# Down in blocks of 1024 features, each replaced in its place, with the block sums of u and W_down made in Up

## The chip, the cores and the metric

The kernel runs on one core of one Trainium2 chip. The metric is the device time of one execution in microseconds; it is 3420.22 us before the change, the median of 3 runs (3415.82 to 3422.02). [...]

## The reference

One layer of an encoder over 2048 rows of 1024 features:

```python
proj = rms_norm(h, g_mix) @ w_in                    # q, k, v of two groups of heads
h = h + concat(diff_attention, dilated_attention) @ w_out
hn = rms_norm(h, g_mlp)
h = h + square(relu(hn @ w_up)) @ w_down            # 1024 -> 4096 -> 1024
gate = sigmoid(rms_norm(h, g_ple) @ w_ple_gate)
h = h + gate * (p @ w_ple_proj)
return rms_norm(h, g_final)
```

The change touches the line with `w_up` and `w_down`, and the edges of the stages beside it.

## The kernel before

The stages run one after the other in one program with hand-written queues for each engine: projection, differential attention, dilated attention, `Mix` (W_out), `Up` (W_up), `Down` (W_down), `Gate`. Semaphores tie the queues; the order of the work on an engine is the order in its queue.

`Up` and `Down` use the Winograd form of Strassen's product: both operands are cut in 2 x 2 blocks, and 7 products of blocks (q = 0 to 6) stand for 8. Some of the 7 operands are blocks as they are, the others are sums and differences of blocks. Each product is made of 3 matmuls for every 128 of the contracted dimension (`matmul3`, lines 136 to 138: hi by hi, hi by lo, lo by hi). ScalarE copies an operand into its hi part (`hi_...`), another engine subtracts that from the operand for the lo part (`lo_...`).

`Up` takes the 2048 rows in two halves (z). The 7 operands of a half (`b_hi`, `b_lo`, made from the transposed rows `xt`, with the sums T1 to T4 in `add_t1` to `add_t4`) stay in SBUF for 16 steps. A step n takes 256 columns of W_up: `load_a` on SP, `sum_a` and `sum_s4` on POOL, `hi_a` on ScalarE, `lo_a` on VectorE, 84 matmuls on TensorE. ScalarE copies three of the products out of PSUM (`copy`) and makes the relu of one block; VectorE adds and squares the others (`y`: lines 1979 and 1981; the y of products 3, 4 and 5 are called y3, y4, y5 here). The four blocks of u = relu squared (u21, u22, u11, u12) are stored to DRAM by SP. Each y of a step waits until all four stores of the step before have landed (`stored`). The seventh product of a step waits for y4.

`Down` contracts the 4096 features. Before the change it takes 512 of them at a time: 2 halves of the rows x 8 groups of features x 2 = 32 passes k. A pass has 7 products q for two pairs of row tiles (s), each of 6 matmuls. u of a group comes in 4 pieces m, in four slots, as four blocks; POOL makes the sums (`sum_u`), ScalarE the hi part and VectorE the lo part of all seven at once. W_down of a group comes as four blocks in one of two slots; POOL makes the sums (`sum_w`), ScalarE the hi parts, VectorE three and POOL four of the lo parts (`lo_w`, line 2154). VectorE adds each product from PSUM to the residual rows `h` in SBUF (`add`, line 2322); TensorE's later products wait for these additions, since they add onto the same bank or reuse it. All DMAs of these stages are issued by SP.

`Gate` follows: W_ple_gate is scaled and split in the last two passes of `Down`.

## Time and profile before

| what | value |
|---|---|
| median of 3 runs | 3420.22 us |
| profiled execution, its own time | 3421.58 us |
| span from first to last instruction | 3419.8 us |
| TensorE matmul busy | 3161.2 us, 92% |
| TensorE weight load busy | 2706.2 us, 79% |
| VectorE busy | 2020.9 us, 59% |
| ScalarE busy | 1418.1 us, 41% |
| POOL (GpSimd) busy | 1396.8 us, 41% |
| granted TensorE clock, mean | 0.977 of full |

Matmuls are pipelined, so the busy time of TensorE adds up durations that overlap: its 0.39 us a matmul is longer than the distance from one to the next. The stages and the waits say more than the shares of the whole span.

### The profile page before, as it was taken

What the parts mean: (1) busy time and instruction counts of PE and PEld (TensorE: products, weight loads), DVE (VectorE), ACT (ScalarE), POOL (GpSimd) and SP (SyncE); (2) the same over time, 40 slices, a digit from 0 to 9 for tenths busy, and PEclk for the clock granted to TensorE, in tenths of its full rate; (3) what the DMA queues carried; (4) which work ended last, traced back from release to release, by engine and by line L of the source; (5) the groups of instructions that cost most, each with busy time, mean ns of one, the idle gap of its engine ahead of it and who ended that gap; (6) DMA issues with size and microseconds to landing.
All of it is one profiled execution on the core that took longest, in us unless ns stands there. A gap on an engine that the chain in (4) does not pass through costs nothing.

```text
span 3419.8 us, 48589 instructions
## 1 busy us (share of the span) xinstructions
PE 3161.2 (92%) x17504; PEld 2706.2 (79%) x17504; DVE 2020.9 (59%) x3415; ACT 1418.1 (41%) x2496; POOL 1396.8 (41%) x1052
## 2 busy tenths in 40 slices
PE   8999999999999999989979998999788868889998
PEld 8988888888888899977868886788676757767787
DVE  5134434888888756655555556555677747776222
ACT  4011112777777778852233333334232213233332
POOL 2133330011111167732342224323788868887322
PEclk9999999999999999999999999999999989999999
DMA  5233337003122168646634332233322242224221
GB/s 176 79 113 123 119 118 182 26 20 82 43 58 71 44 151 208 157 127 223 228 114 137 105 117 103 102 117 124 126 96 99 96 151 99 99 74 152 100 84 53
DMA packets 311341, 384.35 MB, mean 112 GB/s; under 512 B 79552, under 2 KB 225344, under 8 KB 305856
## 3 DMA queue, kind: packets, MB, share of 16 engines
q1 hardware_dynamic: 307760, 374.95, 35.8%
q10 hardware_dynamic: 3344, 6.29, 0.8%
q8 instruction: 142, 2.33, 0.3%
q14 instruction: 95, 0.78, 0.1%
HBM read 254.94 MB, written 126.22 MB: 111 GB/s over the span
## 4 chain that ended last, share of the span: by engine, by line
PE 68%; POOL 14%; DVE 7%; DMA 4%; ACT 4%; issue 3%; SPq 1%; POOLq 0%; DVEq 0%; ACTq 0%
POOL h_w_lo L2154 5%; PE a_acc L136 5%; PE a_acc L137 5%; PE a_acc L138 5%; PE c_pv L844 5%; PE e_acc L136 5%; PE e_acc L137 5%; PE e_acc L138 5%; PE b_pv L984 4%; PE c_turned L833 3%; PE c_scores L825 3%; PE c_scores L826 3%; PE b_scores L1236 3%; DVE c_neg_half L741 2%; DVE c_a_row L774 2%
## 5 line engine op out<-in xcount | busy, mean ns | idle before, releaser
L136 PE MATMUL h_acc<-h_w_hi,h_u_hi 128*128 128x512 f32 x896 | 361.9, 404 | 120.3 <-DVE h_h L2322 120.0
L741 DVE TENSOR_REDUCE c_neg_half<-c_scores 128x1 f32<-128x1024 f32 x256 | 312.7, 1222 | 83.5 <-PE c_scores L826 83.5
L138 PE MATMUL h_acc<-h_w_hi,h_u_lo 128*128 128x512 f32 x896 | 356.8, 398 | 0.0
L137 PE MATMUL h_acc<-h_w_lo,h_u_hi 128*128 128x512 f32 x896 | 356.3, 398 | 0.0
L2322 DVE TENSOR_TENSOR h_h<-h_acc,h_h 128x512 f32<-128x512 f32 x448 | 290.2, 681 | 87.0 <-PE h_acc L138 85.7
L136 PE MATMUL e_acc<-e_b_hi,e_a_hi 128*128 128x512 f32 x768 | 304.0, 396 | 38.0 <-DVE e_u L1979 21.7
L2196 ACT CAST h_u_hi<-h_u_raw 128x1792 fp32r<-128x1792 f32 x64 | 108.5, 1696 | 536.6 <-POOL h_u_raw L2182 536.6
L136 PEld LDWEIGHTS h_acc<-h_w_hi,h_u_hi 128*128 128x128 f32 x896 | 173.0, 193 | 176.3 <-issue 74.2
L698 ACT ACTIVATE c_e<-c_scores,c_neg_max 128x1024 f32<-128x1024 f32 x256 | 287.0, 1121 | 59.7 <-DVE c_neg_max L748 51.8
L137 PE MATMUL e_acc<-e_b_lo,e_a_hi 128*128 128x512 f32 x768 | 303.0, 395 | 0.0
L138 PE MATMUL e_acc<-e_b_hi,e_a_lo 128*128 128x512 f32 x768 | 302.7, 394 | 0.0
L844 PE MATMUL c_pv<-c_v,c_at 128*128 128x128 f32 x2048 | 270.1, 275 | 0.4 <-ACT c_o L712 0.4
L2201 DVE TENSOR_TENSOR h_u_lo<-h_u_raw,h_u_hi 128x1792 fp32r<-128x1792 f32 x64 | 174.7, 2729 | 129.4 <-ACT h_u_hi L2196 129.4
L844 PEld LDWEIGHTS c_pv<-c_v,c_at 128*128 128x128 f32 x2048 | 248.6, 192 | 0.5 <-ACT c_o L712 0.5
L665 POOL TENSOR_SCALAR c_mean<-c_ssq,c_eps 128x1 f32<-128x1 f32 x64 | 16.9, 264 | 546.4 <-ACT c_o_junk L719 515.7
L2154 POOL TENSOR_TENSOR h_w_lo<-h_w_raw,h_w_hi 128x1024 fp32r<-128x1024 f32 x64 | 203.2, 3206 | 84.0 <-ACT h_w_hi L2149 84.0
L825 PE MATMUL c_scores<-c_kt_hi,c_qs 128*128 128x512 f32 x512 | 224.6, 439 | 5.2 <-ACT c_e L698 5.1
L136 PEld LDWEIGHTS e_acc<-e_b_hi,e_a_hi 128*128 128x128 f32 x768 | 146.7, 191 | 71.8 <-DVE e_a_lo L1784 23.7
L826 PE MATMUL c_scores<-c_kt_lo,c_qs 128*128 128x512 f32 x512 | 203.5, 397 | 0.0
L138 PEld LDWEIGHTS h_acc<-h_w_hi,h_u_lo 128*128 128x128 f32 x896 | 172.4, 192 | 37.4
L137 PEld LDWEIGHTS h_acc<-h_w_lo,h_u_hi 128*128 128x128 f32 x896 | 173.4, 194 | 35.2
L706 ACT COPY c_at<-c_turned 128x512 f32<-128x512 f32 x256 | 149.8, 585 | 119.2 <-PE c_turned L833 117.3
(202 smaller groups left out, 8027.4 us busy)
## 6 DMA issues: line engine op xcount, KB each, us to landing
s_qkt<-a_hl SPq DMA_DIRECT2D x128, 256.0 KB, 2.8
e_a<-w_up_dram SPq DMA_DIRECT2D x64, 512.0 KB, 4.9
s_u<-e_u SPq DMA_DIRECT2D x128, 256.0 KB, 2.0
h_w_raw<-w_down_dram SPq DMA_DIRECT2D x64, 512.0 KB, 7.4
h_u_raw<-s_u SPq DMA_DIRECT2D x128, 256.0 KB, 3.4
b_kt<-s_qkt SPq DMA_DIRECT2D x64, 256.0 KB, 9.4
a_w_raw<-w_in_dram SPq DMA_DIRECT2D x24, 512.0 KB, 5.3
d_nd<-s_nd SPq DMA_DIRECT2D x48, 256.0 KB, 3.0
```

The source lines that it names most:

```text
L136: nc.tensor.matmul(out, lhs_hi, rhs_hi, start=first, stop=False, skip_group_check=onto)
L137: nc.tensor.matmul(out, lhs_hi, rhs_lo, start=False, stop=False, skip_group_check=onto)
L138: return nc.tensor.matmul(out, lhs_lo, rhs_hi, start=False, stop=last, skip_group_check=onto)
L698: nc.scalar.activation(e[:, n % 2, m, f * HALF:(f + 1) * HALF], bank(n, u), ACT.Exp, bias=neg_max[:, n % 2, m:m + 1], accum_out=sums[:, n ...
L706: nc.scalar.copy(at[:, n % 2, 4 * g:4 * g + 4].rearrange("p c t -> p (c t)"), turned[:]).then_inc(S["at"], 1)
L741: nc.vector.tensor_reduce(neg_half[:, m, f:f + 1], bank(n, u), AX.X, ALU.max, negate=True).then_inc(S["halved"], 1)
L825: nc.tensor.matmul(found, queries, kt_hi[h % 2][:, m, cols], start=True, stop=False)
L826: ins = nc.tensor.matmul(found, queries, kt_lo[h % 2][:, m, cols], start=False, stop=True)
L844: ins = nc.tensor.matmul(pv[:, :VD], at[:, s, c], v[h % 2][:, c], start=(c == 0), stop=(c == KT - 1))
L2154: op(self.w_lo[s][:, q], self.w_raw[s][:, q], self.w_hi[s][:, q].bitcast(F32), ALU.subtract).then_inc(S[sem], 1)
L2201: self.nc.vector.tensor_tensor(self.u_lo[s][:], self.u_raw[s][:], self.u_hi[s][:].bitcast(F32), ALU.subtract).then_inc(S["u_lo"], 1)
L2322: nc.vector.tensor_tensor(tile, bank[:], tile, ALU.add).then_inc(S["h"], 1)
```

## The change

`Down` takes 1024 features at a time: 4 groups of features, 16 passes, 12 matmuls to a product. There is one place for each of the 7 blocks of W_down and for each of the 7 blocks of u (two parts, s), no second slot. When product q of a pass is done, SP loads the next block of that q into the same place. POOL makes all lo parts of u, VectorE all lo parts of W_down. The additions to `h` are half as many, as a product holds twice the features.

The sums are no longer made in `Down`. In `Up`, POOL makes the block sums of u after u11 and after u12 (`sum_s`, eight operations of 128x256 a step), and SP stores seven blocks in place of four. In steps 18 to 25 of `Up` (`FIRST_T`), SP loads two parts of W_down a step (`load_t`), POOL sums the even and VectorE the odd ones (`sum_t`), and SP stores four sums of each to a new DRAM tensor `t` (`store_t`). The order of the queues in `Up` changes: u12's stores move behind the next step's loads, y4 stands ahead of the first two `lo_a`, T3 is made in the place of a half of `xt` and for the second half of the rows already at step 4, T1 comes from T2 in place too. `Gate` loads W_ple_gate in quarters during the last pass, and its buffers lie elsewhere.

```diff
     def add_t3(self, pool, z):
-        self.free_b(pool, z, 1)
-        self.nc.gpsimd.tensor_tensor(self.b_raw[1][:], self.half(1, 1), self.half(0, 1),
+        pool.wait_ge(self.S["xt_in"], 16 * self.HT * (z + 1))
+        self.nc.gpsimd.tensor_tensor(self.half(0, 1), self.half(1, 1), self.half(0, 1),
                                      ALU.subtract).then_inc(self.S["b_sum"], 1)
...
     def add_t1(self, dve, z):
-        if z == 0:
-            self.mix.wait_products(dve, TILES - 1)
-        self.free_b(dve, z, 4)
-        self.nc.vector.tensor_tensor(self.b_raw[4][:], self.half(0, 1), self.half(0, 0),
+        dve.wait_ge(self.S["b_sum"], 3 * z + 2)
+        dve.wait_ge(self.S["b_lo"], 5 * z + 1)
+        self.nc.vector.tensor_tensor(self.half(0, 0), self.half(1, 1), self.b_raw[2][:],
                                      ALU.subtract).then_inc(self.S["b_t1"], 1)
...
+    def load_t(self, sp, n):
+        for i in range(2):
+            sp.dma_start(self.t[n % 2][:, 2 * i:2 * i + 2].rearrange("p k d -> p (k d)"),
+                         self.D["w_down"][n * 256 + i * P:n * 256 + (i + 1) * P]).then_inc(self.t_in[n % 2], 16)
+
+    def sum_t(self, eng, op, n):
+        S, t, done = self.S, self.t[n % 2], self.t_sum[n % 2]
+        eng.wait_ge(self.t_in[n % 2], 32 * (n // 2 + 1))
+        op(t[:, 4], t[:, 1], t[:, 0], ALU.subtract).then_inc(done, 1)
+        eng.wait_ge(done, 4 * (n // 2) + 1)
+        op(t[:, 5], t[:, 3], t[:, 4], ALU.subtract).then_inc(done, 1)
+        op(t[:, 1], t[:, 3], t[:, 1], ALU.subtract).then_inc(done, 1)
+        eng.wait_ge(done, 4 * (n // 2) + 2)
+        op(t[:, 6], t[:, 2], t[:, 5], ALU.subtract).then_inc(done, 1)
+
+    def store_t(self, sp, n):
+        sp.wait_ge(self.t_sum[n % 2], 4 * (n // 2) + 4)
+        t = self.t[n % 2]
+        sp.dma_start(self.D["t"][n, :, 0], t[:, 1]).then_inc(self.S["t_stored"], 16)
+        sp.dma_start(self.D["t"][n, :, 1:], t[:, 4:]).then_inc(self.S["t_stored"], 16)
...
+    def sum_s(self, pool, n, j):
+        nc, S = self.nc, self.S
+        u1 = (self.u11, self.u12)[j][:].rearrange("p (i k t) -> p i k t", i=2, k=2)
...
+            pool.wait_ge(S["s_stored"], 32 * (2 * n + j))
+        base = 8 * n + 4 * j
+        nc.gpsimd.tensor_tensor(self.s12[:, :, 0], u1[:, :, 1], u2[:, :, 1], ALU.add).then_inc(S["s_sum"], 1)
+        pool.wait_ge(S["s_sum"], base + 1)
+        nc.gpsimd.tensor_tensor(self.s12[:, :, 1], self.s12[:, :, 0], u1[:, :, 0], ALU.subtract).then_inc(S["s_sum"], 1)
+        nc.gpsimd.tensor_tensor(u1[:, :, 1], u1[:, :, 0], u1[:, :, 1], ALU.subtract).then_inc(S["s_sum"], 1)
+        pool.wait_ge(S["s_sum"], base + 2)
+        nc.gpsimd.tensor_tensor(self.s4u[:], u2[:, :, 0], self.s12[:, :, 1], ALU.subtract).then_inc(S["s_sum"], 1)
+
...
+        FIRST_T = range(FB + 2, FB + 2 + FB // 2)
 
...
+            def pairs(n, j, first, last):
                 z, f = divmod(n, FB)
+                return self.D["u"][f, :, 4 * z + 2 * j:4 * z + 2 * j + 2, first:last]
+
...
+            def store_2(n, j, u, y):
                 sp.wait_ge(S["y"], 7 * n + y)
-                cols = slice(z * HT * P + j * 512, z * HT * P + (j + 1) * 512)
-                sp.dma_start(self.D["u"][f, i, :, cols], u[:]).then_inc(S["stored"], 16)
-
-            for n in range(STEPS):
-                if n + 1 < STEPS:
-                    self.load_a(sp, n + 1)
+                sp.dma_start(pairs(n, j, 2, 4), u[:].rearrange("p (i k t) -> p i k t", i=2, k=2)).then_inc(S["stored"], 16)
+
+            def store_1(n, j, u):
+                sp.wait_ge(S["s_sum"], 8 * n + 4 * j + 3)
+                sp.dma_start(pairs(n, j, 0, 2), u[:].rearrange("p (i k t) -> p i k t", i=2, k=2)).then_inc(S["stored"], 16)
+                sp.dma_start(pairs(n, j, 4, 6), self.s12[:]).then_inc(S["s_stored"], 16)
+                sp.wait_ge(S["s_sum"], 8 * n + 4 * j + 4)
+                sp.dma_start(pairs(n, j, 6, 7).rearrange("p i k t -> p i (k t)"), self.s4u[:]).then_inc(S["s_stored"], 16)
+
+            for n in range(STEPS - 1):
+                self.load_a(sp, n + 1)
+                if n == FB + 1:
+                    self.wait_xt_used(sp, 1)
+                if n in FIRST_T:
+                    m = 2 * (n - FIRST_T[0])
+                    if m:
+                        sp.wait_ge(S["t_stored"], 32 * m)
+                    self.load_t(sp, m)
+                    self.load_t(sp, m + 1)
+                if n == FIRST_T[-1] + 1:
+                    self.wait_t(sp)
+                    down.load_w(sp, 0, 0)
+                    down.load_w(sp, 0, 1)
+                if n:
+                    store_1(n - 1, 1, self.u12)
+                store_2(n, 0, self.u21, 2)
+                store_2(n, 1, self.u22, 4)
+                if n in FIRST_T:
+                    self.store_t(sp, m)
+                    self.store_t(sp, m + 1)
+                store_1(n, 0, self.u11)
...
+            n = STEPS - 1
+            store_1(n - 1, 1, self.u12)
+            self.wait_parts(sp)
+            down.load_u(sp, 0, 0)
+            self.wait_product(sp, 0)
+            down.load_w(sp, 0, 2)
+            down.load_u(sp, 0, 1)
+            self.wait_product(sp, 1)
+            down.load_w(sp, 0, 3)
+            self.wait_product(sp, 2)
+            down.load_u(sp, 0, 2)
+            down.load_w(sp, 0, 4)
+            store_2(n, 0, self.u21, 2)
+            self.wait_product(sp, 3)
+            down.load_w(sp, 0, 5)
+            store_2(n, 1, self.u22, 4)
+            self.wait_product(sp, 4)
+            down.load_w(sp, 0, 6)
+            down.load_u(sp, 0, 3)
+            self.wait_product(sp, 5)
+            for t in range(4):
+                down.load_h(sp, 0, t)
+            store_1(n, 0, self.u11)
+            self.wait_product(sp, 6)
+            down.load_u(sp, 0, 4)
+            store_1(n, 1, self.u12)
+            self.wait_last(sp)
+            for t in range(4, HT):
+                down.load_h(sp, 0, t)
+            self.wait_stored(sp)
+            down.load_u(sp, 0, 5)
+            down.load_u(sp, 0, 6)
...
+                    self.lo_b(dve, 1, 1)
                 y(n, 1, 3, self.u21, c, self.u2, 3)
+                y(n, 3, 4, self.u22, a, self.p7, 2)
                 if n == 0:
                     mix.h_out(dve, TILES - 1)
+                    mix.wait_xt(dve, TILES - 1)
+                if n == 0:
+                    y(n, 5, 5, self.u11, self.acc_b[:, 0], self.p1, 1)
                 if n + 1 < STEPS:
-                    self.lo_a(dve, n + 1, 0)
-                    self.lo_a(dve, n + 1, 1)
-                y(n, 3, 4, self.u22, a, self.p7, 2)
-                if n == 0:
-                    mix.wait_xt(dve, TILES - 1)
+                    for q in range(2):
+                        self.lo_a(dve, n + 1, q)
...
+                if n:
+                    y(n, 5, 5, self.u11, self.acc_b[:, 0], self.p1, 1)
                 if n + 1 < STEPS:
-                    for q in range(2, 5):
+                    for q in range(2, 6):
                         self.lo_a(dve, n + 1, q)
...
-                    down.begin_vector(dve, 1)
-                y(n, 5, 5, self.u11, self.acc_b[:, 0], self.p1, 1)
-                if n + 1 < STEPS:
-                    self.lo_a(dve, n + 1, 5)
                 square(n)
...
                 if n + 1 < STEPS:
                     self.lo_a(dve, n + 1, Q - 1)
+                if n in FIRST_T:
+                    self.sum_t(dve, nc.vector.tensor_tensor, 2 * (n - FIRST_T[0]) + 1)
...
-            for n in range(STEPS - 1):
-                if n + 1 == FB:
-                    self.add_t3(pool, 1)
-                self.sum_a(pool, n + 1)
+            for n in range(STEPS):
                 if n + 1 == FB:
                     self.add_t2(pool, 1)
                     self.add_t4(pool, 1)
-                if n == FB + 6:
-                    down.sum_w(pool, 0)
-                self.sum_s4(pool, n + 1)
-            down.begin_pool(pool)
+                if n + 1 < STEPS:
+                    self.sum_a(pool, n + 1)
+                else:
+                    down.begin_pool(pool)
+                if n == 4:
+                    self.add_t3(pool, 1)
+                if n in FIRST_T:
+                    self.sum_t(pool, nc.gpsimd.tensor_tensor, 2 * (n - FIRST_T[0]))
+                self.sum_s(pool, n, 0)
+                if n + 1 < STEPS:
+                    self.sum_s4(pool, n + 1)
+                self.sum_s(pool, n, 1)
...
-    HALVES, HT, FG = 2, TILES // 2, D_FF // 512
+    HALVES, HT, FG = 2, TILES // 2, D_FF // 1024
     GROUPS = HALVES * FG
     DPS = GROUPS * 2
-    PAIRS_Z = HT // 2
-    SLOTS = 4
-    Q = 7
+    Q, J = 7, 4
...
+        homes = (0, 16, 32, 48, 124.25, 140.25, 156.25)
+        self.w_raw = [place(kit, f"h_w_raw{q}", kb, [P, J, 512]) for q, kb in enumerate(homes)]
+        self.w_lo = [place(kit, f"h_w_lo{q}", kb, [P, J, 512], F32R) for q, kb in enumerate(homes)]
+        self.w_hi = [place(kit, f"h_w_hi{q}", kb + 8, [P, J, 512], F32R) for q, kb in enumerate(homes)]
+        homes = ((68, 72), (76, 188.5), (192.5, 196.5), (80, 84), (88, 92), (112, 116), (120, 64))
+        self.u_raw = [[place(kit, f"h_u_raw{q}_{s}", kb, [P, J, P]) for s, kb in enumerate(h)] for q, h in enumerate(homes)]
+        self.u_lo = [[place(kit, f"h_u_lo{q}_{s}", kb, [P, J, P], F32R) for s, kb in enumerate(h)] for q, h in enumerate(homes)]
+        self.u_hi = [[place(kit, f"h_u_hi{q}_{s}", kb + 2, [P, J, P], F32R) for s, kb in enumerate(h)]
...
+    def load_w(self, sp, r, q):
+        f = self.J * (r % self.FG)
+        if r:
+            self.wait_product(sp, 2 * r - 1, q, 1)
+        s, before = self.loads(r, q)
+        if before:
+            sp.wait_ge(self.w_in[s], 16 * before)
+        if q in (0, 5, 6):
+            i, k = (q + 1) // 7 + (q == 5), int(q == 6)
+            src = self.D["w_down"].rearrange("(f i p) d -> f i p d", i=2, p=P)[f:f + self.J, i, :, k * 512:(k + 1) * 512]
...
+            src = self.D["t"][f:f + self.J, :, (0, 2, 3, 1)[q - 1]]
+        sp.dma_start(self.w_raw[q][:], src.rearrange("j p d -> p j d")).then_inc(self.w_in[s], 16)
+
+    def hi_w(self, act, r, q):
+        s, before = self.loads(r, q)
+        act.wait_ge(self.w_in[s], 16 * before + 16)
+        self.nc.scalar.copy(self.w_hi[q][:], self.w_raw[q][:]).then_inc(self.S["w_hi"], 1)
+
+    def lo_w(self, dve, r, q):
+        dve.wait_ge(self.S["w_hi"], self.Q * r + q + 1)
+        self.nc.vector.tensor_tensor(self.w_lo[q][:], self.w_raw[q][:], self.w_hi[q][:].bitcast(F32),
+                                     ALU.subtract).then_inc(self.S["w_lo"], 1)
+
+    def load_u(self, sp, k, q):
+        f, half = self.J * (k // 2 % self.FG), 4 * (k // (2 * self.FG)) + 2 * (k % 2)
+        if k:
+            self.wait_product(sp, k - 1, q, 1)
+        n, before = self.loads(k, q)
+        if before:
+            sp.wait_ge(self.u_in[n], 32 * before)
+        for s in range(2):
+            sp.dma_start(self.u_raw[q][s][:], self.D["u"][f:f + self.J, :, half + s, self.POS[q]].rearrange("j p t -> p j t")
+                         ).then_inc(self.u_in[n], 16)
+
+    def hi_u(self, act, k, q, s):
+        n, before = self.loads(k, q)
+        act.wait_ge(self.u_in[n], 32 * before + 32)
+        self.nc.scalar.copy(self.u_hi[q][s][:], self.u_raw[q][s][:]).then_inc(self.S["u_hi"], 1)
+
+    def lo_u(self, pool, k, q, s):
+        pool.wait_ge(self.S["u_hi"], 14 * k + 2 * q + s + 1)
+        self.nc.gpsimd.tensor_tensor(self.u_lo[q][s][:], self.u_raw[q][s][:], self.u_hi[q][s][:].bitcast(F32),
+                                     ALU.subtract).then_inc(self.S["u_lo"], 1)
...
+                r, step = k // 2, k % (2 * FG)
+                for q in range(Q):
+                    if k + 1 < DPS:
+                        self.load_u(sp, k + 1, q)
+                    else:
+                        self.wait_product(sp, k, q, 1)
+                        gate.load_early(sp, q)
+                    if k % 2 and r + 1 < GROUPS:
+                        self.load_w(sp, r + 1, q)
+                    if q == 2 and 0 < k - 2 * FG + 2 < 3:
+                        first = 4 * (k - 2 * FG + 1)
+                        for t in range(first, first + 4):
+                            self.load_h(sp, 1, t)
...
+            for k in range(DPS - 1):
+                for q in range(Q):
+                    for s in range(2):
+                        self.hi_u(act, k + 1, q, s)
+                    if k % 2:
+                        self.hi_w(act, k // 2 + 1, q)
+            for c in range(KC):
+                gate.split_hi(act, c)
...
+                for q in range(Q):
+                    if k == 0 and q + 2 < Q:
+                        self.lo_w(dve, 0, q + 2)
+                    for s in range(2):
+                        add(k, q, s)
+                    if k % 2 and r + 1 < GROUPS and q >= 2:
+                        self.lo_w(dve, r + 1, q - 2)
+                    if k % 2 == 0 and k and q < 2:
+                        self.lo_w(dve, r, q + 5)
...
+            for k in range(DPS - 1):
                 for q in range(Q):
                     for s in range(2):
...
+                        self.lo_u(pool, k + 1, q, s)
+            for c in range(KC):
+                gate.split_lo(pool, c)
...
+                pe.wait_ge(S["u_lo"], 14 * k + 2 * q + s + 1)
...
+                for j in range(J):
+                    ins = matmul3(nc, out[:], self.u_hi[q][s][:, j], self.u_lo[q][s][:, j],
+                                  self.w_hi[q][:, j], self.w_lo[q][:, j], q in (0, 1, 5) and j == 0, j == J - 1,
+                                  q not in (0, 1, 5))
...
+    def load_early(self, sp, q):
+        if q < 4:
+            self.load_w(sp, q)
+        if q == 0:
+            self.load_h(sp, 0)
+            self.load_h(sp, 1)
+        elif q == 1:
+            sp.dma_start(self.e_raw[1][:], self.D["w_ple_proj"][P:]).then_inc(self.e_in, 16)
+            self.load_h(sp, 2)
...
+        elif q == 3:
+            self.load_h(sp, 3)
```

## Rows read from the trace of the kernel before

**Rows 1.** The windows view of Up and Down; its first line names the columns.

```profile
core 0: us, PE busy (x) PEld busy (x) DVE busy (x) ACT busy (x) POOL busy (x), PEclk, DMA share, GB/s
1757.60:2398.60 641.00, 603.51 (x2615) 496.83 (x2616) 370.92 (x452) 223.69 (x357) 207.96 (x143) 0.97 0.35 119
2398.60:3163.50 764.90, 644.58 (x2698) 515.39 (x2696) 521.42 (x558) 219.64 (x182) 611.48 (x376) 0.96 0.32 110
```

**Rows 2.** POOL's timeline in Up: s4, begun as a step's products end.

```profile
2044.92 1.29 POOL L1767 TENSOR_TENSOR e_s<-e_a 128x512 f32<-128x512 f32 x1 [6.95 <-PE e_acc L138]
...
2103.84 1.29 POOL L1767 TENSOR_TENSOR e_s<-e_a 128x512 f32<-128x512 f32 x1 [7.38 <-PE e_acc L138]
...
2199.04 1.29 POOL L1767 TENSOR_TENSOR e_s<-e_a 128x512 f32<-128x512 f32 x1 [6.90 <-PE e_acc L138]
...
2242.88 1.74 POOL L1767 TENSOR_TENSOR e_s<-e_a 128x512 f32<-128x512 f32 x1 [4.41 <-PE e_acc L138]
...
2376.16 1.50 POOL L1767 TENSOR_TENSOR e_s<-e_a 128x512 f32<-128x512 f32 x1 [6.45 <-PE e_acc L138]
```

**Rows 3.** The waits in Down: total us, times, longest.

```profile
ACT h_u_hi L2196 <- POOL h_u_raw L2182: 532.3, 62, 26.9
...
PE h_acc L136 <- DVE h_h L2322: 120.0, 50, 15.0
```

**Rows 4.** POOL's timeline in Down, one round of a group.

```profile
2830.73 0.75 POOL L2177 TENSOR_TENSOR h_u_raw<-h_u_raw 128x256 f32<-128x256 f32 x1
...
2841.07 12.70 POOL L2154 TENSOR_TENSOR h_w_lo<-h_w_raw,h_w_hi 128x1024 fp32r<-128x1024 f32 x4 [5.60 <-ACT h_w_hi L2149]
...
2875.57 0.74 POOL L2177 TENSOR_TENSOR h_u_raw<-h_u_raw 128x256 f32<-128x256 f32 x1
```

**Rows 5.** TensorE's timeline: Up's start, and after a stall in Down.

```profile
1772.44 0.76 PE L136 MATMUL e_acc<-e_b_hi,e_a_hi 128*128 128x512 f32 x1 [15.38 <-DVE e_u L1979]
...
2817.42 0.63 PE L137 MATMUL h_acc<-h_w_lo,h_u_hi 128*128 128x512 f32 x1
2817.84 0.63 PE L138 MATMUL h_acc<-h_w_hi,h_u_lo 128*128 128x512 f32 x1
```

**Rows 6.** Instructions grouped by line and shape: busy us, mean ns, idle before.

```profile
L2322 DVE TENSOR_TENSOR h_h<-h_acc,h_h 128x512 f32<-128x512 f32 x448 | 290.2, 681 | 87.0 <-PE h_acc L138 85.7
L1847 DVE TENSOR_TENSOR e_b_lo<-e_b_raw,e_b_hi 128x2048 fp32r<-128x2048 f32 x5 | 11.3, 2283 | 0.9 <-ACT e_b_hi L1840 0.9
L1840 ACT CAST e_b_hi<-e_b_raw 128x2048 fp32r<-128x2048 f32 x5 | 9.5, 1904 | 11.2 <-DVE e_b_raw L1815 5.7 <-POOL e_b_raw L1802 2.8 <-POOL e_b_raw L1794 2.7
L1757 POOL TENSOR_TENSOR e_a<-e_a 128x512 f32<-128x512 f32 x31 | 41.5, 1340 | 229.3 <-DMA e_a<-w_up_dram 229.3
L2154 POOL TENSOR_TENSOR h_w_lo<-h_w_raw,h_w_hi 128x1024 fp32r<-128x1024 f32 x64 | 203.2, 3206 | 84.0 <-ACT h_w_hi L2149 84.0
L2139 POOL TENSOR_TENSOR h_w_raw<-h_w_raw 128x1024 f32<-128x1024 f32 x16 | 38.5, 2405 | 1.3
L2177 POOL TENSOR_TENSOR h_u_raw<-h_u_raw 128x256 f32<-128x256 f32 x64 | 48.1, 752 | 56.0 <-DMA h_u_raw<-s_u 56.0
```

**Rows 7.** DMA: a store alone and 1775 to 1800; loads, 1781 to 1796, 2762 to 2768.

```profile
s_u<-e_u SPq DMA_DIRECT2D x128, 256.0 KB, 2.0
...
s_u<-e_u SPq DMA_DIRECT2D x6, 256.0 KB, 5.2
...
DMA packets 7312, 4.21 MB, mean 281 GB/s; under 512 B 124, under 2 KB 7311, under 8 KB 7311
...
DMA packets 1120, 2.28 MB, mean 380 GB/s; under 512 B 89, under 2 KB 723, under 8 KB 1119
```

**Rows 8.** SP's timeline, and two of its issue lines (ns min/median/max).

```profile
1760.22 1.38 SPq L1750 DMA_DIRECT2D e_a<-w_up_dram  x2
...
2047.62 0.93 SPq L1750 DMA_DIRECT2D e_a<-w_up_dram  x2
...
L1892 SPq DMA_DIRECT2D s_u<-e_u x10: 319/338/339, 2116.4 to 2157.3; - x10
...
L2132 SPq DMA_DIRECT2D h_w_raw<-w_down_dram x64: 373/470/1543, 2126.6 to 3076.6; - x64
```

375 lines of the change are left out of this document (110 added, 265 removed).

## The prediction

> **What bounds the kernel now.** I read the three last stages by their windows first, then the waits inside the slowest, then the timeline of the engine those waits name. Up (32 steps) takes 641.0 us, Down (32 passes) 764.9 us, and TensorE issues about as many matmuls in both [rows 1]. Up's undisturbed pace is seen between two of its POOL rows seven steps apart: (2376.16 - 2242.88)/7 = 19.04 us a step of 84 matmuls, 0.2267 us each [rows 2]. Down has 2688 matmuls too, so at that pace it would take 609.3 us. It loses 155.6 us, and nothing but waits can be the cause: TensorE waits 120.0 us for VectorE's h_h additions, and those queue behind h_u_lo, behind ScalarE's h_u_hi, which waited 532.3 us for POOL's sums of u [rows 3]. The second set of u sums of one group starts at 2830.73 and the same set of the next at 2875.57: POOL goes round in 44.84 us where two passes need 38.07 [rows 4]. Four h_w_lo alone are 12.70 us of it. So POOL bounds Down, with further stalls (the longest 15.0 us) at the start and where the halves change, and the matmuls after a long stall run at half pace (0.42 us apart, the lower of the clock's two levels) [rows 5].
>
> **Down after the change.** It has 16 passes of 168 matmuls, again 2688. A pass is 168 x 0.2267 = 38.1 us.
> POOL: all sums go; it makes 14 u_lo of 128x512 per pass. The nearest rows are 128x512 sums at 1.34 us and 128x1024 lo parts at 3.21, 1.6 per 512 [rows 6]: 19 to 23 us. Not a bound.
> VectorE: 14 additions x 0.68 = 9.5 us, and seven w_lo of 128x2048 in every second pass, 2.28 us each, 16.0 us [rows 6]: 25.5 of 38.1. Additions halve from 448 to 224.
> ScalarE: 14 u_hi at 0.6 (a quarter of the 1.90 for 128x2048, and 0.1 for what doesn't shrink) and seven w_hi at 1.90 [rows 6]: 22 us.
> DMA: a pass loads 3.67 MB of u in 512 B pieces and, every second pass, 7.34 MB of W in 2 KB pieces. Loads with 512 B pieces moved 4.21 MB in 15 us, 281 GB/s; pieces of 1 to 4 KB 380 GB/s [rows 7]. So 13.1 + 19.3 = 32.4 us of a 38.1 us pass, 13 in the other. Each block's place is free after its product, and the next block is wanted there 12 products later, 12 x 2.72 = 32.6 us; load 4.7 + 2, hi 3, lo 4 need some 14. If VectorE's w_lo waits for a late block, the additions behind it have 8 us (three products) before TensorE misses them.
> Entry: u blocks 5 and 6 must wait for the last stores, but are wanted only at +27 us. Blocks of q = 2 wait on POOL behind the last sum of u, and this behind stores queued after 2 MB of h: at about +13 against +10.9. I take 5 us, and 2 for the rest. Down: 609.3 + 7 = 616, **-149 us** (bounds: 0 more, and +40 if each of the 8 odd passes slips 5 us).
>
> **Up, the stalls that go.** At the start VectorE holds y4 behind lo_a(1), whose W_up load issues at 1760.22, and TensorE waits 15.38 us [rows 5, 8]. With y4 ahead, TensorE does the seventh product and waits then for the same load, landing near 1768, lo part 1769: step 1 starts near 1769 instead of 1775: -6. At the change of halves two steps take 58.92 us instead of 38.08 [rows 2], 20.8 lost to T3, T2, T4 on POOL and their split. T3 is made at step 4 and its hi and lo early; T2 and T4 still wait for products, T4 ends near +18 us of the step, sum_a behind it at +22, ScalarE's relu behind those at +26, where +21.8 was due: 5 us, with slow clock 8: -12. The POOL sum of W (2199.04 to 2242.88, 43.84 for 38.08) goes: -6. The last step: -2. Together **-26 us** (0 to -35).
>
> **Up, the stalls that come.** POOL gets eight sums of 128x256 a step at 0.75 (a quarter of a 1024's 2.4 to 3.2): 6 us beside 5.4. s4 now follows the sums of u11 (done near +3), so s4 is ready at +4.3, its lo part at +5.7, and load_a, which waits for it, issues near +5.8 of a step; u12's store follows it, lands near +11.3, and y3, due at +10.9, may start until 14.1 before TensorE waits. I take 0 for ordinary steps (bound +3 each over 20 steps).
> In steps 18 to 25 SP's queue closes a circle. y3 of step n+1 (and all y behind it) waits for all four stores of step n. u12's store stands behind load_t of step n+1; load_t waits until the t sums of step n have landed; their odd half waits for VectorE's sum_t. That is last in VectorE's step n, behind the lo part of s4: it runs in step n+1 after s4 (+4.3), hi and lo (+5.7) and its own four operations (4 x 0.8), near +9. Count from its end, E. SP: two t stores 0.9, three stores of u 1.0, two load_a 0.93 [rows 8]: 2.9. 1 MB of t lands at 0.5 + 1.3 + 2.7 = 4.5 (2.7 for 1 MB at 380 GB/s; 1.3 is what is left of a small store's 2.0 without its 0.7 of bytes). Four load_t issue until 6.4, 0.47 each [rows 8]. By then 2.74 MB were issued ahead and drain at +8.1, 2.1 MB of load_t at +13.5; u12's store lands near +15. y3 0.7, its square 1.1, y4 0.7: +17.6. y4's square, two lo_a, y5: +21. POOL sums u11: +24; s4: +25.2; hi and lo: +26.8; sum_t 4 x 0.8: +30. The circle is 30 us, not 19.04: +11 for seven turns. TensorE feels it at the seventh product of a step, due at 16.3 and let go at 9 + 17.6 = 26.6; step 26, with 2 MB of W_down in the same place, pays 10 once more, plus 2 for the slow clock: **+89 us**.
> What decides is whether a small store waits for loads issued before it. A store of u lands in 2.0 us alone; in the stretch with eight xt loads the six stores had a median of 5.2 [rows 7]. That shows queueing, though not its full length, since these stores were issued with only part of the 4 MB still outstanding. I take full queueing, for this is the only stretch of before in which a store follows megabytes of loads. The Trainium skill ("DMA: Bandwidth & Descriptors", Queues, rings and completion order) says that a ring's descriptors are consumed in order and that the semaphore's increment lands only after every earlier write of that DMA engine. By that rule u12 lands when load_t is in, so the term is +89; by a store that lands as fast as alone it would be +37.
> Bounds: if stores pass loads, u12 lands at 2.9 + 1.6 + 2 + 2.3 = 8.8, the circle is 24: 5 x 7 + 2 = +37. If VectorE and POOL hold each other up (h_w_lo 3.21 beside 2.4), 35 us: 16 x 7 + 16 = +128.
>
> **Gate.** This only moves. Its W comes in quarters in the last pass, at 5.4, 10.9, 16.3 and 21.8 us of it; ScalarE needs some 2 us (twice half of the 1.90) and POOL up to 3.2 for each of eight chunks [rows 6]; the last two, in near +29, are done near +36. Tiles 2 and 3 of h2 load earlier, worth at most the first few us: -2 (bounds -5 and 0).
>
> **Sum.** -149 - 26 + 89 - 2 = -88. The profiled execution took 3421.58 us (span 3419.8): 3333.6. The median of the runs, 3420.22, is 1.4 less: **3332 us**.
>
> **Rivals.**
> A, the t stores cost little: stores pass loads, or the landing is faster. For it: DMA peaks at 380 GB/s and is idle most of a step. Against: the queueing seen above. Circle at 24 us or no circle: 3420 - 177 + 37 = 3280, or 3243 with none.
> B, ordinary steps slip too: with 1.5 to 3 us of stall each over some 20 steps (u12's store later than 14.1), +30 to +60: 3362 to 3392. For it: VectorE's operations stretch beside POOL's. Against: 2.8 us of margin.
> C, slower: Down becomes bound by loads. u comes in 512 B pieces 28 KB apart, which no row has on the read side (xt's pieces were small on the chip's side alone). It must eat 88 us: 5.9 us a pass more, (616 + 95)/16 = 44.4; a pair moves 14.7 MB, so the queue would have to manage under 165 GB/s. Against: 281 to 380 in rows [rows 7]. Break-even is 88 us lost there; at 155 to 165 GB/s it gives 3430 to 3480.
> D, the change doesn't lift POOL's bound because VectorE waits for late w_lo and so TensorE for sums, 3 to 5 us a pass: +50 to +80, 3382 to 3412; the 8 us margin speaks against.
>
> **Chances.** Forecast 0.60, A 0.17, B 0.11, C 0.06, D 0.06. The range reaches to A's 3280 and a little under, and to B's upper part: 3275 to 3385. The measurement tells no change within 0.2%, 7 us. Faster 0.92, same 0.02, slower 0.06.
>
> **What would show it.** Down from first to last h_acc near 616 us, no wait of h_acc for h_h over 3 us, POOL under 65% there. Steps 19 to 26 near 30 us, others 19.04; there y3 waiting for a store of u, and load_t issued some 4.5 us after the last t store. Halves change with under 10 us lost. I am wrong if steps 19 to 26 stay at 19 to 22 us (A), if steps 5 to 14 grow (B), or if in Down h_u_hi waits for loads (C) or h_acc for h_h behind h_w_lo (D).

## The result, and the profile after

The changed kernel takes **3453.88 us**, the median of 4 runs (3451.6 to 3456.27), against 3419.75 for the kernel before (4 runs): a ratio of 1.0101, 95% interval 1.0084 to 1.0119. It is slower by 34 us, 1%, where 3332 was forecast. The profiled execution has a span of 3449.8 us, 30.0 more than before. I read the same views again, first the windows of Up and of Down (the columns are those of [rows 1]):

```profile
1757.00:2564.70 807.70, 638.77 (x2605) 511.11 (x2606) 443.98 (x478) 210.58 (x353) 488.98 (x409) 0.90 0.49 165
2564.70:3197.20 632.50, 613.00 (x2697) 507.08 (x2695) 290.53 (x278) 246.10 (x299) 406.56 (x240) 0.98 0.68 217
```

Down falls by 132.4 us against [rows 1], close to the -149 forecast. Up grows by 166.7 where +63 was forecast. What follows gives 3.7 back, what precedes 0.6: -132.4 + 166.7 - 3.7 - 0.6 = +30.0. So the question is Up. TensorE's waits in the changed kernel (total us, times, longest):

```profile
PE e_acc L136 <- DVE e_u L2077: 107.1, 13, 12.8
PE e_acc L136 <- ACT e_p L2016: 50.8, 28, 9.7
...
PE h_acc L136 <- POOL h_u_lo L2274: 19.5, 1, 19.5
PE e_acc L136 <- DVE e_a_lo L1789: 12.3, 3, 7.8
```

The first is the large wait at the seventh product that the prediction expected in a few steps. The second is short, 1.8 us on average, but comes 28 times: nearly every step. POOL's timeline gives the pace, s4 of steps 5, 15, 19 and 27, as [rows 2] did:

```profile
1873.10 1.71 POOL L1772 TENSOR_TENSOR e_s<-e_a 128x512 f32<-128x512 f32 x1
...
2086.69 1.74 POOL L1772 TENSOR_TENSOR e_s<-e_a 128x512 f32<-128x512 f32 x1
...
2196.02 1.74 POOL L1772 TENSOR_TENSOR e_s<-e_a 128x512 f32<-128x512 f32 x1
...
2461.00 1.74 POOL L1772 TENSOR_TENSOR e_s<-e_a 128x512 f32<-128x512 f32 x1
```

Ordinary steps: (2086.69 - 1873.10)/10 = 21.36 us, not 19.04. Steps with t: (2461.00 - 2196.02)/8 = 33.12 us, not 30. These rows also lack the "<-PE e_acc" of [rows 2]: POOL no longer begins s4 as a step's products end, it comes to it late, and s4 itself takes 1.72 instead of 1.29 us. From the distances of all 32 of these rows in both kernels, the increase of Up by part (us):

| part of Up | forecast | measured |
|---|---|---|
| start, up to s4 of step 1 | -6 | -6.1 |
| step 2 (eight loads of xt) | 0 | +13.3 |
| 18 ordinary steps | 0 | +46.5 |
| the two steps at the change of halves | -12 | +2.9 |
| steps 18 to 26 (t), with the POOL sum of W that goes | +83 | +114.2 |
| rest | -2 | -4.1 |

### The profile page after: what moved, and what is told of

It is laid out like the page before. It is cut to its first block, busy times and chain, and to the rows that moved or that the text cites. A ratio compares the mean times of both kernels' runs of the same rounds, so it can differ in the third digit from the quotient of the medians.

```text
span 3449.8 us, 48933 instructions
## 1 busy us (share of the span) xinstructions
PE 3165.3 (92%) x17504; PEld 2711.1 (79%) x17504; DVE 1868.5 (54%) x3167; ACT 1424.7 (41%) x2600; POOL 1463.6 (42%) x1180
## 4 chain that ended last, share of the span: by engine, by line
PE 68%; DVE 9%; DMA 8%; POOL 7%; issue 5%; SPq 2%; ACT 1%; DVEq 0%; POOLq 0%; ACTq 0%
PE h_acc L136 6%; PE h_acc L137 6%; PE h_acc L138 6%; PE a_acc L137 5%; PE a_acc L138 5%; PE a_acc L136 5%; PE c_pv L844 5%; DMA s_u<-e_u 4%; PE b_pv L984 4%; PE c_turned L833 3%; PE b_scores L1236 3%; PE c_scores L825 2%; PE c_scores L826 2%; DVE c_neg_half L741 2%; DVE c_a_row L774 2%
## 5 line engine op out<-in xcount | busy, mean ns | idle before, releaser
L136 PE MATMUL e_acc<-e_b_hi,e_a_hi 128*128 128x512 f32 x768 | 318.8, 415 | 172.7 <-DVE e_u L2077 107.1
L2274 POOL TENSOR_TENSOR h_u_lo<-h_u_raw,h_u_hi 128x512 fp32r<-128x512 f32 x224 | 378.2, 1713 | 209.3 <-ACT h_u_hi L2270 209.3
L136 PE MATMUL h_acc<-h_w_hi,h_u_hi 128*128 128x512 f32 x896 | 350.0, 391 | 19.5 <-POOL h_u_lo L2274 19.5
L2368 DVE TENSOR_TENSOR h_h<-h_acc,h_h 128x512 f32<-128x512 f32 x224 | 154.1, 689 | 330.8 <-PE h_acc L138 318.3
L137 PE MATMUL e_acc<-e_b_lo,e_a_hi 128*128 128x512 f32 x768 | 313.2, 408 | 0.0
L2270 ACT CAST h_u_hi<-h_u_raw 128x512 fp32r<-128x512 f32 x224 | 127.5, 617 | 259.1 <-DMA h_u_raw<-s_u 259.0
L1783 ACT CAST e_a_hi<-e_a 128x512 fp32r<-128x512 f32 x192 | 110.2, 618 | 254.4 <-DMA e_a<-w_up_dram 143.6
L136 PE MATMUL a_acc<-a_xt_hi,a_w_hi 128*128 128x512 f32 x512 | 199.2, 389 | 0.0
L137 PE MATMUL a_acc<-a_xt_lo,a_w_hi 128*128 128x512 f32 x512 | 199.2, 389 | 0.0
L138 PE MATMUL a_acc<-a_xt_hi,a_w_lo 128*128 128x512 f32 x512 | 199.2, 389 | 0.0
```

What stands on the lines that cost most here:

```text
L136: nc.tensor.matmul(out, lhs_hi, rhs_hi, start=first, stop=False, skip_group_check=onto)
L137: nc.tensor.matmul(out, lhs_hi, rhs_lo, start=False, stop=False, skip_group_check=onto)
L138: return nc.tensor.matmul(out, lhs_lo, rhs_hi, start=False, stop=last, skip_group_check=onto)
L2270: self.nc.scalar.copy(self.u_hi[q][s][:], self.u_raw[q][s][:]).then_inc(self.S["u_hi"], 1)
L2274: self.nc.gpsimd.tensor_tensor(self.u_lo[q][s][:], self.u_raw[q][s][:], self.u_hi[q][s][:].bitcast(F32), ALU.subtract).then_inc(self.S["u_ ...
L2368: nc.vector.tensor_tensor(tile, bank[:], tile, ALU.add).then_inc(S["h"], 1)
```

## The experiments

All runs are of one execution, except the changed kernel and the timed one below. The kernel before, run beside them, took 3411.91 to 3428.04 us in nine executions of one session and 3414.7, 3415.94 and 3422.22 in the others. So a difference of some 10 us between two single runs proves little by its total; there the distances and waits in the traces decide. "Pace" is the mean distance of the s4 rows in steps 5 to 14 (ordinary); for the steps with t the text names the steps. The runs that leave out t or its sums compute another product; they serve as measurements of time alone.

**The copy.** TensorE's short waits are for ScalarE's first copy of a step. This copy stands behind hi of s4, and hi of s4 waits for POOL's late s4. Edit: the copy goes ahead of hi of s4.

```diff
                 copy(n, 1, 0, self.p1, a, 5)
+                if n:
+                    self.hi_a(act, n, Q - 1)
...
-                if n + 1 < STEPS:
-                    self.hi_a(act, n + 1, Q - 1)
```

> ScalarE takes the first copy of a step (product 0 out of PSUM) ahead of the hi part of s4. Theory A (order of queues): an ordinary step of Up takes 21.4 us instead of 19.04 because that copy stands behind the hi part of s4, which waits for POOL's sums of u11; with the copy ahead, ordinary steps fall to 19.0 to 19.6 us, some 40 us over Up (3454 to about 3412), while steps 19 to 26 stay near 33 us. Rival B (POOL and VectorE are simply too full in Up): ordinary steps stay above 21 us, and TensorE waits for another releaser instead.

3453.59 us, pace 21.4: no change, as rival B had it. TensorE's wait moves from e_p to e_u, since now y3 is what is late:

```profile
1992.39 0.69 DVE L2077 TENSOR_TENSOR e_u<-e_acc,e_u 128x512 f32<-128x512 f32 x1 [6.64 <-DMA s_u<-e_u]
```

So the copy was a symptom, and there is a chain that returns to itself once a step. It is seen in the changed kernel, step 9 to 10 (start, duration, engine):

```profile
1953.28 1.12 POOL L1901 TENSOR_TENSOR e_s<-e_u,e_u 128x256 f32<-128x256 f32 x1 [3.16 <-DVE e_u L2079]
...
1956.65 1.19 POOL L1906 TENSOR_TENSOR e_s4u<-e_u,e_s 128x256 f32<-128x256 f32 x1
...
1957.80 1.72 POOL L1772 TENSOR_TENSOR e_s<-e_a 128x512 f32<-128x512 f32 x1
...
1959.55 0.62 ACT L1783 CAST e_a_hi<-e_s 128x512 fp32r<-128x512 f32 x1 [5.44 <-POOL e_s L1772]
...
1960.19 0.72 POOL L1901 TENSOR_TENSOR e_s<-e_u,e_u 128x256 f32<-128x256 f32 x1 [0.67 <-DMA s_u<-e_s4u]
1960.20 1.26 DVE L1789 TENSOR_TENSOR e_a_lo<-e_s,e_a_hi 128x512 fp32r<-128x512 f32 x1 [1.82 <-ACT e_a_hi L1783]
...
1961.49 1.08 SPq L1755 DMA_DIRECT2D e_a<-w_up_dram  x2
...
1962.02 0.73 POOL L1904 TENSOR_TENSOR e_u<-e_u 128x256 f32<-128x256 f32 x1
...
1962.77 0.37 SPq L1944 DMA_DIRECT2D s_u<-e_u  x1
...
1968.20 0.69 DVE L2077 TENSOR_TENSOR e_u<-e_acc,e_u 128x512 f32<-128x512 f32 x1 [6.74 <-DMA s_u<-e_u]
...
1974.14 0.69 DVE L2079 SCALAR_TENSOR_TENSOR e_u<-e_u 128x512 f32<-128x512 f32 x1
...
1974.91 1.12 POOL L1901 TENSOR_TENSOR e_s<-e_u,e_u 128x256 f32<-128x256 f32 x1 [3.16 <-DVE e_u L2079]
```

Read it downwards: POOL's first sums of u (4.5 us), s4, its hi and lo, the load of a that waits for that lo, u12's store behind the load, y3 that waits for the store to land (5.4 us after its issue), y4, two lo parts and y5, and POOL's sums of the next step: 21.63 us round. Beside it runs a second branch: POOL's second sums wait for s4 and then for the landing of the first sums' stores, and u12's store waits for the third of them. The two branches end together: SP is free at 1962.57, the third sum is done at 1962.75, and the store goes at 1962.77. The wait for the landing is only 0.67 us here, since s4 covers the rest.

**The loads of xt.** Step 2 has the same wait in large. y3 waits 19.50 us for u12's store, which stands in SP's queue behind eight 512 KB loads (seven of them in the first row) and the two loads of a:

```profile
1794.45 10.88 SPq L1748 DMA_DIRECT2D e_xt<-s_xt  x7
...
1805.38 4.01 SPq L1755 DMA_DIRECT2D e_a<-w_up_dram  x2
1809.43 0.83 SPq L1944 DMA_DIRECT2D s_u<-e_u  x1
```
```profile
1815.66 0.69 DVE L2077 TENSOR_TENSOR e_u<-e_acc,e_u 128x512 f32<-128x512 f32 x1 [19.50 <-DMA s_u<-e_u]
```

POOL's sums for this store are done at 1798.2. It is issued 11 us later, as SP is busy issuing the loads until then, and y3 starts 6.2 us after its issue. Edit: the loads one iteration later, behind u12's store.

```diff
                 store_1(n, 0, self.u11)
-                if n == 1:
...
-                        self.load_xt(sp, 1, t)
...
+                if n == 2:
...
+                        self.load_xt(sp, 1, t)
                 store_2(n, 0, self.u21, 2)
```

> The eight loads of xt for the second half are issued behind u12's stores of step 1 instead of ahead of them. If a small store waits for the loads issued before it, step 2 falls from 33.7 us to 21 to 24 us and the whole gets 10 to 13 us faster. If the queue of loads is not what holds VectorE there, step 2 stays near 33 us or the loss moves to step 3 in full.

3441.22 us, -12.7; step 2 falls from 33.7 to 20.5 us. This is the term that the forecast lacked.

**Down's entry.** TensorE waits 19.5 us for lo parts of u that stand on POOL behind the last sum of u, and this waits for stores that SP issues late:

```profile
2587.77 1.93 POOL L1901 TENSOR_TENSOR e_s<-e_u,e_u 128x256 f32<-128x256 f32 x1 [16.87 <-DMA s_u<-e_s4u]
```

Edit: the sum behind the lo parts of blocks 2 and 3.

```diff
                 if n + 1 < STEPS:
                     self.sum_s4(pool, n + 1)
-                self.sum_s(pool, n, 1)
+                    self.sum_s(pool, n, 1)
...
             for q in range(2, Q):
+                if q == 4:
+                    up.sum_s(pool, up.STEPS - 1, 1)
                 for s in range(2):
                     self.lo_u(pool, 0, q, s)
```

> On POOL the last sum of u moves behind the lo parts of u blocks 2 and 3 of Down. Theory: the 19.5 us that TensorE waits in Down's first pass are POOL waiting 16.9 us for a store with two lo parts queued behind it; they fall to under 6 us, and the whole gets 12 to 18 us faster. Rival: the loads of block 2 and 3 themselves come late; then the wait only falls by 5 us, and h_acc waits for later blocks (u blocks 5 and 6, which need the last stores).

3444.7 us, -9, and not the 12 to 18 expected. The wait of 19.5 us becomes one of 7.7 us for VectorE's first addition, with 4.1 left of the old one:

```profile
PE h_acc L136 <- DVE h_h L2368: 7.7, 1, 7.7
PE h_acc L136 <- POOL h_u_lo L2274: 4.1, 2, 3.9
```

**No t.** Edit: the loads, sums and stores of t go; Down loads plain blocks of W_down in their place.

```diff
-                    self.load_t(sp, m)
-                    self.load_t(sp, m + 1)
...
-                    self.store_t(sp, m)
-                    self.store_t(sp, m + 1)
...
-                    self.sum_t(dve, nc.vector.tensor_tensor, 2 * (n - FIRST_T[0]) + 1)
...
-                    self.sum_t(pool, nc.gpsimd.tensor_tensor, 2 * (n - FIRST_T[0]))
```

> Leaves out the block sums of W_down (no loads, sums and stores of t; Down loads plain blocks of W_down in their place, so its product is another one). Theory A: steps 18 to 26 fall from 26.4 and 33.1 us to the 21.4 us of ordinary steps: 8 x 11.7 + 5 = 99 us faster, 3355 us. Rival B (steps 18 to 26 are slow because POOL and VectorE are full there, and would be without the store in the queue): the same. So this run gives the price of the whole part; what it tells apart is whether Down (632.5 us) changes when its blocks all come from W_down: by theory A it stays within 3 us.

3352.55 us: 101 us less. Steps 18 to 25 fall to ordinary ones (21.2), Down stays within 0.5 us of 632.5. So the t part costs 101 us in a kernel whose ordinary steps take 21 us, and those stay.

**u12's store ahead of t's work.** Edit:

```diff
+                if n:
+                    store_1(n - 1, 1, self.u12)
                 if n == FB + 1:
                     self.wait_xt_used(sp, 1)
                 if n in FIRST_T:
...
-                if n:
-                    store_1(n - 1, 1, self.u12)
                 store_2(n, 0, self.u21, 2)
```

> Edit: in SyncE's queue the stores of u12 and its sums stand ahead of the loads of W_down's tiles (t), not behind them; nothing else. In the changed kernel steps 19 to 26 take 33.1 us each. Theory 1 (the circle of these steps runs through u12's store, which waits behind 4 loads of t, lands 7.7 us after its issue and lets y3 start 16.5 us late): the stores land some 6 us earlier, the steps fall to 26 to 28 us, the whole to about 3405. Theory 2 (the circle is POOL's own order: the sums of t, then both sums of u, each beside VectorE's work, and the t stores of the step before gate the loads): the loads of t start later by POOL's sum_s of the step before, which is what y3's gain is given back for; steps stay at 31 to 34 us, the whole 3440 to 3460. Ordinary steps stay at 21.3 us in both.

3436.41 us; steps 19 to 25 take 31.7 us where the changed kernel takes 33.3: theory 2. What the prediction named as the deciding link, a store queued behind 2 MB of loads, is worth 1.6 us of the 14 a step. What then holds the steps is tried next, by changing the waits for t's stores.

**The order of t.** Edit, with the one before: VectorE's tile is stored in the next step, and each of the two buffers has its own count.

```diff
+                if n - 1 in FIRST_T:
+                    self.store_t(sp, m - 1)
                 if n in FIRST_T:
-                    if m:
-                        sp.wait_ge(S["t_stored"], 32 * m)
-                    self.load_t(sp, m)
-                    self.load_t(sp, m + 1)
+                    for k in range(2):
+                        if m:
+                            sp.wait_ge(self.t_out[k], 16 * m)
+                        self.load_t(sp, m + k)
...
                     self.store_t(sp, m)
-                    self.store_t(sp, m + 1)
                 store_1(n, 0, self.u11)
```

> The changed kernel with POOL's sums of u as they are; of the t part: u12's stores ahead of all t work, the stores of VectorE's tile of t in the next step behind them, and each t buffer loaded as soon as its own stores have landed. Steps 19 to 26 took 33.1 us, 31.7 with u12's stores ahead alone. Theory (the circle of these steps is POOL's sum of t 5.3 to 7 us and its first sums of u behind it, which wait for the loads of t, which wait for VectorE's stores of t of the step before): the load of POOL's tile starts up to 8 us earlier, and the steps fall to 24 to 27 us, the whole to 3454 - 8 x 7 = about 3398. Rival (VectorE's and POOL's sums beside each other, whatever the order, make these steps): 30 to 32 us, the whole 3435 to 3445.

3394.3 us, and s4 of steps 19 and 27:

```profile
2195.84 1.26 POOL L1772 TENSOR_TENSOR e_s<-e_a 128x512 f32<-128x512 f32 x1
...
2404.70 1.74 POOL L1772 TENSOR_TENSOR e_s<-e_a 128x512 f32<-128x512 f32 x1
```

Steps 19 to 26 take 26.1 us, 19 to 25 alone 26.7: 5.0 us more are gone. The kernel so far had two orders that this run undoes together: SP held u11's stores back until VectorE's late sum of t was done, and the load of POOL's tile until both tiles' stores had landed. Together they cost three times what the place of u12's store did; what each is worth alone no run shows.

**Who makes the sums of u.** Three runs without t, to be compared with the run without t above (3352.55 us, pace 21.0). First: `sum_s` on VectorE, u11's behind lo of block 3 and u12's behind the last lo.

```diff
                         self.lo_a(dve, n + 1, q)
+                self.sum_s(dve, n, 0)
...
                     self.lo_a(dve, n + 1, Q - 1)
+                self.sum_s(dve, n, 1)
...
-                self.sum_s(pool, n, 0)
                 if n + 1 < STEPS:
                     self.sum_s4(pool, n + 1)
-                self.sum_s(pool, n, 1)
```

> Leaves out the sums, loads and stores of W_down's tiles (as the fourth experiment, 3352.55 us, whose Down takes plain blocks of W_down); beside that, the sums of u's blocks are made by VectorE: those of u11 behind lo of block 3, those of u12 behind the last lo part. Ordinary steps took 21.3 us with POOL's sums. Theory 1 (ordinary steps are bound by the second circle y5, POOL's first sums 4.5 us beside VectorE, their stores, POOL's second sums, u12's store, y3): the sums take some 0.4 us each on VectorE, all of them stores some 3 to 5 us earlier, the steps fall to 19.0 to 19.5 us, the whole to about 3352 - 25 x 2 = 3300. Theory 2 (the steps are bound by VectorE's own list y3, y4, lo, y5): 3.5 us more on VectorE a step make them 22 to 24 us, the whole 3365 to 3400.

3289.96 us, -63, as theory 1 had it: eight of the ten ordinary steps take 19.0. So POOL's sums of u are what makes the ordinary steps longer. Next: POOL keeps the sums, but in steps 18 to 24 the second ones have buffers of their own.

```diff
+    SET = range(18, 25)
+
+    def set(self, n, j):
+        return (self.s12b, self.s4ub) if j and n in self.SET else (self.s12, self.s4u)
...
```

> Leaves out the t part as the one before; beside that, in steps 18 to 24 the second sums of a step (those of u12) go to a second pair of buffers, so that POOL doesn't wait until the first ones' stores have landed; in the other steps nothing changes, which is the comparison within one run. Theory 1a (the wait for the first sums' stores, 2.2 us and more a step, stands in the circle): steps 18 to 24 fall from 21.2 to about 19.0 to 19.5 us, the others stay, the whole about 3352 - 13 = 3339. Theory 1b (SyncE can't issue u12's store before its own work ahead of it is done, so POOL's wait is covered): steps 18 to 24 as the others, the whole 3350 to 3355.

3362.97 us, nearest to theory 1b: steps 18 to 24 take 20.9 us, 21.2 without the edit; the other ordinary steps 21.8. The wait that the edit takes away was small to begin with. POOL waited for these stores 37.3 us in the whole run without t, 16.4 of them at Down's entry, and 0.7 us a step otherwise, since it makes s4 while they land. (The 120.3 us of the changed kernel stand mostly in the steps with t: 88.1 us in steps 19 to 26, 6.8 in steps 5 to 14.) In this run 33.1 us are left, again 17.2 of them at the entry:

```profile
POOL e_s L1914 <- DMA s_u<-e_s4u: 33.1, 24, 17.2
```

So this run can't tell whether the second branch would bind without s4 in it.

Third: u12's stores ahead of the loads of a.

```diff
+                if n:
+                    store_1(n - 1, 1, self.u12)
                 self.load_a(sp, n + 1)
...
-                if n:
-                    store_1(n - 1, 1, self.u12)
                 store_2(n, 0, self.u21, 2)
```

> Leaves out the t part as the fourth experiment (3352.55 us, ordinary steps 21.2 us); beside that, in SyncE's queue u12's stores of a step stand ahead of the loads of a of the step after the next, not behind them. Theory (the circle of an ordinary step is: y5, POOL's first sums 4.5 us, s4 behind them, its hi and lo, the load of a that waits for that lo, u12's store behind the load, landing 5 us after its issue with 1 MB ahead, y3 that waits for it): u12's stores start some 1.3 us earlier at best or wait for POOL's second sums, and land some 2 to 2.5 us after their issue; the steps fall to 19.0 to 20.2 us, the whole to 3310 to 3330. Rival (the loads of a, now 1 to 2 us later, set hi and lo of block 0 and 1, which stand ahead of y5): steps 21 to 22 us, the whole 3350 to 3365.

3424.01 us (the kernel before took 3422.22 beside it), 23.8 a step, worse than theory and rival. y3 now waits for TensorE alone. But the loads of a stand behind POOL's second sums now; my reading of the order is that the circle closes through lo of block 1 and y5 and is longer. In this one queue the store takes its place from the load.

**s4 elsewhere.** The kernel with the second buffers (its expectation calls it the seventh), with s4 made by VectorE.

```diff
-                if n + 1 < STEPS:
-                    self.sum_s4(pool, n + 1)
...
+                if n + 1 < STEPS:
+                    self.sum_s4(dve, n + 1)
                 square(n)
```

> Leaves out the t part, as the fourth and seventh experiments. Against the seventh (two pairs of sum buffers in steps 18 to 24; all its steps 21.2 us) one edit: s4 is made by VectorE behind the four lo parts, so that it doesn't stand behind POOL's first sums of u. So in steps 2 to 14 the first circle's branch (first sums 4.5 us, s4 1.7, hi, lo, load of a) is cut and the other one (first sums, their stores' landing, second sums, u12's store) stands, and in steps 18 to 24 both are cut. Theory (two branches of nearly one length, each enough for 21 us): steps 2 to 14 take 20.5 to 21.5 us, steps 18 to 24 take 19.0 to 19.8; the whole about 3335 to 3345. Rival (it is only that s4 stands behind the sums): 19.0 to 19.5 in both; about 3310. Second rival (POOL's and VectorE's ops beside each other are what lasts): 21 us in both; about 3360.

3322.31 us, and both sorts of steps are shorter; s4 of steps 5, 15, 18 and 25:

```profile
1872.92 1.22 DVE L1777 TENSOR_TENSOR e_s<-e_a 128x512 f32<-128x512 f32 x1
...
2070.87 1.22 DVE L1777 TENSOR_TENSOR e_s<-e_a 128x512 f32<-128x512 f32 x1
...
2150.52 1.22 DVE L1777 TENSOR_TENSOR e_s<-e_a 128x512 f32<-128x512 f32 x1
...
2289.32 1.22 DVE L1777 TENSOR_TENSOR e_s<-e_a 128x512 f32<-128x512 f32 x1
```

The mean is 19.80 us in steps 5 to 14, where the second sums still wait for the first ones' stores, and 19.83 in steps 18 to 24, where they don't. So the landing of these stores adds nothing, my theory of two branches of nearly one length is wrong, and the first rival is right, in size not quite (19.0 to 19.5). To have s4 off POOL is worth 1.1 to 2.0 us a step. One step shows where the gain lies:

```profile
1948.15 1.12 POOL L1917 TENSOR_TENSOR e_s<-e_u,e_u 128x256 f32<-128x256 f32 x1 [3.16 <-DVE e_u L2089]
...
1954.67 1.08 SPq L1757 DMA_DIRECT2D e_a<-w_up_dram  x2
1955.07 0.74 POOL L1917 TENSOR_TENSOR e_s<-e_u,e_u 128x256 f32<-128x256 f32 x1 [2.36 <-DMA s_u<-e_s4u]
...
1957.35 0.37 SPq L1961 DMA_DIRECT2D s_u<-e_u  x1
...
1960.83 0.69 DVE L2087 TENSOR_TENSOR e_u<-e_acc,e_u 128x512 f32<-128x512 f32 x1 [6.19 <-DMA s_u<-e_u]
```

Counted from the start of POOL's first sums, u12's store is issued at 9.20 us here and at 9.49 in the changed kernel: hardly earlier, since the wait for the landing, now 2.36 us, takes the place of s4. But y3 starts 3.48 us after that issue instead of 5.43, and the loads of a are issued 2.7 us ahead of the store instead of 1.3. That the store lands sooner because these loads are further on fits; no run varies this distance alone. What is left over 19.04, 0.8 us, is gone only in the run with all sums of u on VectorE.

**Versions that beat both.** These do the whole computation. First: the sums of u on VectorE, t's order as above, the loads of xt later (the edits shown, joined).

> The whole computation, with: the sums of u on VectorE; the stores of u12 ahead of all t work in SyncE's queue; each of the two t buffers with its own count of stores, so that a buffer is loaded as soon as its own stores have landed; VectorE's tile of t stored in the next step, behind u12's stores; the loads of the second half of x behind u12's stores. Theory (the three circles are what was lost in Up): ordinary steps 19.2, steps with t 21 to 24 us (6.8 MB each at the 281 to 380 GB/s that rows show is 18 to 24 us), Down unchanged with 632 us or 620 without POOL's late sum ahead of the lo parts: 3454 - 50 (ordinary) - 80 (t) - 12 (x) - 12 (entry) = about 3300. Rival (VectorE becomes the bound: 3.5 us of sums more in each step and 3 to 4 us of t): ordinary 21 to 22, t steps 26 to 28, the whole 3370 to 3400.

3327.07 us, between the theory's 3300 and the rival's 3370; steps 18 to 25 take 24.4 us, and Down's entry has a new wait of 16.0 us for VectorE's first addition. Then with the first copy ahead, and u11's last store ahead of the loads of h:

```diff
             store_2(n, 0, self.u21, 2)
+            store_1(n, 0, self.u11)
             self.wait_product(sp, 3)
...
                 down.load_h(sp, 0, t)
-            store_1(n, 0, self.u11)
```

> The eighth experiment's kernel (3327.1 us; steps with t 24.5 us with a wait of 5.0 us for ScalarE's first copy; 16.0 us for VectorE's first sum of Down) with two edits: ScalarE's first copy of a step ahead of hi of s4, and u11's last stores ahead of the loads of h. Theory: the 5.0 us wait goes or falls under 1.5 us, the steps with t fall to 20 to 22 us (7 x 3 = -21), the wait of 16.0 goes (-14): about 3292. Rival (these steps are bound by what the queues carry, 27.8 MB in 98 us with the DMA share at 0.84; the wait moves to y3): 24 us stay, about 3312.

3307.95 us. Steps 18 to 25 stay at 24.6, and the wait for the copy becomes one for y3, as the rival said. The gain is elsewhere, among others in the change of halves (57.0 to 53.0) and Down's entry (16.0 to 9.6). Then VectorE's y3 and y4 ahead of the lo parts of x (shown), and, not shown, ScalarE's hi parts of x between copies, POOL's s4 ahead of its sum of t, and the stores of this sum in the next step:

```diff
-                if switch:
-                    self.lo_b(dve, 1, 0)
-                    self.lo_b(dve, 1, 1)
                 y(n, 1, 3, self.u21, c, self.u2, 3)
                 y(n, 3, 4, self.u22, a, self.p7, 2)
+                if switch:
+                    self.lo_b(dve, 1, 0)
+                    self.lo_b(dve, 1, 1)
...
```

> The same as the one before with two edits more: at the change of halves VectorE does y3 and y4 ahead of the first two lo parts of x's second half (y3 stood 9.3 us late behind them, one op of 128x256 took 4.83 us beside a POOL op of 4.80), and ScalarE makes the last four hi parts between the copies of the next step (4.8 us wait); in the steps with t POOL makes s4 ahead of its sum of t, whose stores move to the next step. Theory: the two steps at the change fall from 57.0 to some 45 us; the steps with t as before or 1 us less: about 3280. Rival (VectorE's total work in the two steps decides, so that the wait only moves): 55 us stay; and the later stores of t make the steps with t longer, 26 us: 3305 to 3315.

3318.89 us. The change of halves takes 57.6 (24.4 + 33.2): the wait moved to the second step, as the rival had it, and nothing is gained. The second of these versions, timed:

> The eleventh experiment's kernel again (3307.95 us in one run), timed: sums of u on VectorE, u12's stores ahead of all t work, each t buffer loaded as soon as its own stores have landed and VectorE's tile stored in the next step, the loads of x behind u12's store, ScalarE's first copy ahead of hi of s4, u11's last store early. Expected 3308 +- 5, which is 0.967 of the kernel before and 0.958 of the changed one.

**3314.35 us** (5 runs, 3309.51 to 3320.06): a ratio of 0.9694 to the kernel before (nine executions, median 3419.55), interval 0.9672 to 0.9716. The single run of 3307.95 was below all five, and the median is 1.4 us above the expected range. Up and Down there, and TensorE's largest wait:

```profile
1757.00:2433.00 676.00, 617.29 (x2601) 501.22 (x2600) 525.41 (x725) 211.82 (x352) 255.01 (x161) 0.96 0.59 195
2433.00:3067.00 634.00, 621.25 (x2730) 513.43 (x2729) 294.36 (x292) 246.91 (x299) 399.60 (x234) 0.99 0.69 223
```
```profile
PE e_acc L136 <- DVE e_u L2079: 41.4, 15, 6.4
```

Up is 132 us shorter than in the changed kernel, with the same work in it. VectorE is busy 81 us longer there, POOL 234 us less.

**What the steps with t still cost.** The sums of t go; tiles are loaded and stored as before, so Down works on plain blocks in place of sums.

```diff
-        sp.wait_ge(self.t_sum[n % 2], 4 * (n // 2) + 4)
+        sp.wait_ge(self.t_in[n % 2], 32 * (n // 2 + 1))
         t = self.t[n % 2]
         sp.dma_start(self.D["t"][n, :, 0], t[:, 1]).then_inc(self.t_out[n % 2], 16)
-        sp.dma_start(self.D["t"][n, :, 1:], t[:, 4:]).then_inc(self.t_out[n % 2], 16)
+        sp.dma_start(self.D["t"][n, :, 1:], t[:, 1:4]).then_inc(self.t_out[n % 2], 16)
```

> The eleventh experiment's kernel (3307.95 us; its steps with t 24.6 us) without the sums of W_down's tiles: the tiles are loaded and four blocks of each are stored as before, but they are the plain blocks, so that Down works on wrong blocks of the same size. Theory 1 (what is left above 19 us in these steps is the sums: 2.8 us on VectorE, and POOL's beside VectorE's, whose ops of 128x256 take 1.5 us there instead of 0.42): the steps fall to 19.0 to 20.5 us, the whole to about 3270. Theory 2 (it is the transfers, 6.8 MB a step): they stay at 23 to 25 us, the whole at 3300 to 3310.

3286.38 us, 16 more than theory 1 has. Steps 18 to 25 fall from 24.6 to 20.4 us, which is in its range. Windows of 175 us there, without the sums (first) and in the timed version:

```profile
2145.00:2320.00 175.00, 166.12 (x720) 135.48 (x720) 117.42 (x189) 56.76 (x95) 46.34 (x33) 0.99 0.96 333
```
```profile
2155.00:2330.00 175.00, 147.81 (x590) 118.07 (x588) 146.44 (x182) 44.10 (x78) 83.81 (x57) 0.92 0.84 285
```

Without the sums the DMA share is 0.96 at 333 GB/s: at 20 us a step the DMA engines have hardly anything left, so the transfers of theory 2 would be the next bound.

## Why the prediction was wrong

**Down: mechanism right.** 14 lo parts of u, seven w_lo and half the additions fit under TensorE's 38.1 us a pass, and h_acc waited for h_h nowhere. The lo parts cost more than I took (1.72 us each for u where I had 1.34 to 1.6, 2.68 for W where I had 2.28) and still fit: POOL is busy 64% of Down. Rivals C and D didn't come. The sign that I named for C did: ScalarE's h_u_hi waits for loads 63 times, 255.4 us in all. But it was ahead of what TensorE needed, which after the entry waited for nothing, so the sign was badly chosen. The term that was off is the entry: 5 us forecast, 19.5 measured. I had the chain (block 2 behind POOL's last sum behind SP's stores), but not that SP needs 4.04 us for one pair of load_u and 3.57 for four of h there, so that u11's stores are issued at 2576.86.

**"I take 0 for ordinary steps" is the step that failed, with 46 us.** I counted the same chain, found u12's store landed near +11.3 and 2.8 us of margin, and took that as cover. Three things were wrong. First, sums at 0.75 us and s4 at 1.29 are what POOL needs alone. Here the sums take 1.1 to 1.2 and s4 1.72; VectorE's four lo parts run beside the sums and take 4.12 us together instead of 2.5. Second, I had u12's store follow the loads of a at once. In fact it also waits for three of POOL's second sums, which stand behind s4 and the landing of the first ones' stores. Counted from the first sum, which I put at the start of a step, the loads go at +8.2 instead of +5.8, the store at +9.5, and y3 starts at +14.9, where I had the store landed at +11.3. Third, I took each step to begin on time. The chain doesn't return to TensorE but to POOL's own sums, through y3, y4 and y5, so the margin isn't new in each step. How much of the 2.3 us a step is owed to the longer operations and how much to the order, no run separates: with the sums on VectorE both go. Rival B named the place and priced it at 1.5 to 3 us a step, and 2.6 came in the 18 ordinary steps (2.3 in steps 5 to 14). It had 0.11, and its total, 3362 to 3392, was missed too. The measured time lies in the 3430 to 3480 of rival C, but by luck: C's mechanism, a Down bound by loads, didn't come.

**Steps with t: +114 where +83 stood.** Of the 31 us, 23 lie in the seven turns (33.3 us each, not 30) and 7 in step 18, for which I had nothing. The circle exists and is as described; y3 starts 16.5 us after the end of the sum of t (15 forecast), load_t is issued 5.1 after (4.5). The trace of the changed kernel, from that end (2201.66) to the next (2234.15), 32.5 us:

```profile
2201.69 0.32 SPq L1890 DMA_DIRECT2D s_t<-e_t  x1
...
2206.81 2.11 SPq L1874 DMA_DIRECT2D e_t<-w_down_dram  x4
...
2210.42 0.38 SPq L1944 DMA_DIRECT2D s_u<-e_u  x1
...
2218.14 0.69 DVE L2077 TENSOR_TENSOR e_u<-e_acc,e_u 128x512 f32<-128x512 f32 x1 [16.48 <-DMA s_u<-e_u]
...
2228.51 1.73 POOL L1772 TENSOR_TENSOR e_s<-e_a 128x512 f32<-128x512 f32 x1
...
2233.47 0.68 DVE L1885 TENSOR_TENSOR e_t<-e_t 128x512 f32<-128x512 f32 x1
```

This turn is 2.5 us longer than my 30. y3 is 1.5 us late, and POOL adds 2.0: four sums in 4.5 us instead of 3, s4 in 1.73 instead of 1.29. VectorE's sums of t were quicker than I took (0.68 us each, not 0.8), which gives some back. u12's store lands 7.7 us after its issue here, behind 3 MB of loads, where a store alone took 2.0. The Trainium skill's rule on it ("DMA: Bandwidth & Descriptors", Queues, rings and completion order) agrees. But this link was not what decides: with the store ahead of the loads of t the steps only shorten from 33.3 to 31.7 us, and the order of t's own stores and loads gave 5.0.

**The change of halves: -12 forecast, +3 measured.** VectorE's operations take far longer beside POOL's T sums of 128x2048: the squares of y3 and y4, 0.69 us alone, take 4.02 and 4.34. The kernel before has this at one square (4.37 us, y4's) and at three lo parts of a (7.30 together). So the order that I changed put a second one beside them. That it makes the whole 15 us isn't shown; moving y3 and y4 in the last of the versions only moved the wait.

```profile
2094.35 6.64 POOL L1807 TENSOR_TENSOR e_b_raw<-e_xt 128x2048 f32<-128x2048 f32 x1
```
```profile
2097.53 4.02 DVE L2079 SCALAR_TENSOR_TENSOR e_u<-e_u 128x512 f32<-128x512 f32 x1
```

**Step 2: +13, not seen.** The change puts u12's store behind the next step's loads. I followed the 1 MB of a there, and the 2 MB of t, but not the 4 MB of xt, although I used that very stretch as evidence that a store queues.

The start (-6.1 for -6) was right, and what follows Down (-3.7 for -2) nearly. The sum of the misses: 46 + 31 + 15 + 13 in Up, less 2 for its start and rest, 17 in Down, less 2 for what lies around: 118. The other 4 of the 122 us between 3332 and 3454 lie between the medians and the profiled executions, 1.4 above the median before and 2.3 below it after.

## What to carry to other kernels

Work moved from a stage whose bound is an engine to one whose bound is TensorE isn't free because the engines there are half idle: ask what it stands ahead of in their queues, and whether that chain ends in an engine's own next turn. A margin within one step covers nothing if each step starts from the last one's end; the period of the circle is what counts, with durations as the engines have them beside each other. When a wait is removed and another of the same size appears, follow what releases it until a name repeats: here it took moving the new sums themselves, or s4 behind them, and not the copy, the buffers or the store. And before you remove a wait, read how long it is in the very steps in question: the one for the buffers was 0.7 us there, though its total over the kernel was 120.

## What the runs showed of the hardware that I had not expected

- POOL and VectorE stretch each other when both work SBUF to SBUF, and VectorE the more the longer POOL's operation is. VectorE's 128x256 sum takes 0.42 us alone, 1.5 beside POOL's 128x512 sums of t, and 4.83 beside one of 128x2048 (in the first of the whole versions):

```profile
2058.38 4.80 POOL L1807 TENSOR_TENSOR e_b_raw<-e_xt 128x2048 f32<-128x2048 f32 x1 [6.65 <-issue]
2058.63 4.83 DVE L1906 TENSOR_TENSOR e_s4u<-e_u,e_s 128x256 f32<-128x256 f32 x1
```

  Both end within 0.3 us of each other. An addition of 128x512 with one input in PSUM kept its 0.68 us beside POOL's T sum (at 2101.47 in the changed kernel). The Trainium skill ("SBUF — State Buffer", SBUF: two separate sides) has it that VectorE's operations with two SBUF inputs and POOL's lock one pair of ports for a whole instruction, and the later one blocks. The rows agree: the sum that began 0.25 us after POOL's took 4.83 us beside POOL's 4.80.
- The same 128x256 sum is 0.42 us on VectorE and 0.73 on POOL alone, 1.1 to 1.2 beside VectorE.
- SP's time for one issue isn't constant: at Down's entry two loads of u took 1.05 us and, 3.5 us later, 4.04; the two loads of a took 1.1 us in an ordinary step and 4.0 behind the eight loads of xt.
- TensorE's granted clock over Up was 0.90 of full in the changed kernel, with waits of up to 12.8 us, 0.97 in the kernel before, and 0.99 in the stretch where the steps ran at 20 us.
